# Gated delta net, chunk matrices: the values' factor on ScalarE, the rate's factor of the lower matrix on GpSimd a stage earlier

## The reference, cut to what matters

```python
decay = jnp.exp(jnp.where(incl, gc[..., :, None] - gc[..., None, :], -jnp.inf))
kb = k * beta[..., None]
vb = v * beta[..., None]
L = jnp.where(strict, jnp.einsum('bhncd,bhnsd->bhncs', kb, k) * decay, 0.0)
T = lax.linalg.triangular_solve(eye + L, eye, left_side=True, lower=True, unit_diagonal=True)
u = T @ vb
w = T @ (kb * jnp.exp(gc)[..., None])
a_intra = jnp.where(incl, jnp.einsum('bhncd,bhnsd->bhncs', q, k) * decay, 0.0)
kd = k * jnp.exp(gc[..., -1:] - gc)[..., None]
```

## Time and profile before

| | |
|---|---|
| median of 3 runs | 2669.14 us (2658.22 to 2669.57) |
| profiled execution | 2671.5 us, span 2669.5 us |
| instructions | 44222 |
| TensorE busy | 2329.7 us, 87% of the span |
| VectorE busy | 1002.1 us, 38% |
| ScalarE busy | 448.7 us, 17% |
| GpSimd busy | 243.8 us, 9% |
| mean granted TensorE clock | 0.93 of full speed |

### The profile page before, as it was taken

The page is one execution under the profiler, slowest core; times in us unless marked ns, Lnnn a source line. Parts: engine busy times, 40 slices in busy tenths (PEclk is TensorE's granted clock), DMA queues, the critical chain, the costliest instruction groups (busy, mean ns, idle before and its releaser), DMA issues. The chain is left out here.

```text
span 2669.5 us, 44222 instructions
## 1 busy us (share of the span) xinstructions
PE 2329.7 (87%) x18735; PEld 1249.5 (47%) x18735; DVE 1002.1 (38%) x1791; ACT 448.7 (17%) x841; POOL 243.8 (9%) x180
## 2 busy tenths in 40 slices
PE   7989958969898995896986997879979979999998
PEld 3543417634364441862433442379744444444442
DVE  1166685332116667523224452274331152111112
ACT  1021431010102142101021333212110020000000
POOL 0112210000011221000001560210000000000000
PEclk9989979979899997997987998889989979999999
DMA  4111050020212105002011101100104239999997
GB/s 151 52 63 65 16 209 3 22 80 32 91 52 71 63 9 209 3 22 79 32 63 40 48 17 52 67 3 5 34 33 150 107 151 406 421 421 422 422 422 312
DMA packets 60439, 328.25 MB, mean 123 GB/s; under 512 B 6880, under 2 KB 9440, under 8 KB 31200
## 3 DMA queue, kind: packets, MB, share of 16 engines
q1 hardware_dynamic: 60256, 325.63, 31.4%
HBM read 320.88 MB, written 4.72 MB: 122 GB/s over the span
## 5 line engine op out<-in xcount | busy, mean ns | idle before, releaser
L418 PE MATMUL ps<-store,side_ring 128*128 128x512 f32 x928 | 454.4, 623 | 22.5 <-DMA side_ring<-in_w_rwkv 6.3
L418 PEld LDWEIGHTS ps<-store,side_ring 128*128 128x128 f32 x928 | 166.8, 195 | 205.7 <-issue 179.8
L2192 PE MATMUL ps<-expert_ring,xe 128*64 128x512 f32 x1024 | 223.3, 593 | 2.8 <-DVE back L2301 1.7
L333 PE MATMUL ps<-store,side_ring 128*128 128x512 f32 x384 | 170.9, 608 | 1.9 <-DVE store L299 1.9
L2192 PEld LDWEIGHTS ps<-expert_ring,xe 128*64 128x64 f32 x1024 | 73.0, 137 | 149.6 <-issue 147.5
L333 PEld LDWEIGHTS ps<-store,side_ring 128*128 128x128 f32 x384 | 74.8, 196 | 96.9 <-issue 94.8
L1447 PE MATMUL ps<-store,weight_ring 128*128 128x512 f32 x256 | 112.0, 593 | 1.9 <-DVE store L299 1.9
L2220 PE MATMUL ps<-expert_ring,store 128*64 128x512 f32 x512 | 111.6, 594 | 1.4 <-DVE store L2277 1.4
L1962 PE MATMUL ps<-store,expert_ring 128*128 128x512 f32 x224 | 98.9, 605 | 10.8 <-DMA expert_ring<-in_w_merge 10.8
L546 DVE COPY attn_tok<-ps 128x456 f32<-128x456 f32 (+1 forms) x12 | 6.2, 519 | 237.3 <-PE ps L536 237.3
L418 PE MATMUL ps<-store 128*128 128x512 f32 x160 | 80.1, 656 | 13.7 <-DMA store<-in_w_merge 13.2
(11 more groups left out here) (406 smaller groups left out, 3875.2 us busy)
## 6 DMA issues: line engine op xcount, KB each, us to landing
expert_ring<-in_w_expert SPq DMA_DIRECT2D x192, 1024.0 KB, 16.4
raw<-in_w_ada SPq DMA_DIRECT2D x24, 1024.0 KB, 6.5
side_ring<-in_w_attn SPq DMA_DIRECT2D x34, 512.0 KB, 3.7
side_ring<-in_w_rwkv SPq DMA_DIRECT2D x26, 512.0 KB, 3.6
weight_ring<-in_ple_gate SPq DMA_DIRECT2D x16, 512.0 KB, 3.7
side_ring<-in_w_conv SPq DMA_DIRECT2D x12, 512.0 KB, 3.3
store<-in_w_merge SPq DMA_DIRECT2D x10, 512.0 KB, 3.7
expert_ring<-in_w_merge SPq DMA_DIRECT2D x3, 1536.0 KB, 6.4
```

The source lines that it names most:

```text
L333: last = nc.tensor.matmul(ps[:, u, :], ring[:, u, k, :], src[:, k, :], start=(k == 0), stop=(k == kt - 1))
L418: ins = self.nc.tensor.matmul(self.ps[:, self.banks[j % banks], :], self.ring[:, j % self.slots, k, :], self.src[:, k, :], start=(k == 0), ...
L2192: last = nc.tensor.matmul(ps[w, 2 * ep + half, :], xe[:, ep, k, :], ring[:, unit % SLOTS, k2, S * half:S * half + S], start=(k == 0), stop ...
```

## The change

In the stage of the decays GpSimd waits for its own mask of chunk `n` and then multiplies `low` of that chunk by the rate, broadcast along the columns (semaphore `by_beta`). In the stage of the chunk matrices ScalarE gets a program: per chunk, direction and pair of heads it copies 128x64 of the value bank into `bv` with the rate as its scale, one pair of heads per instruction (semaphore `v_scaled`), and TensorE waits for both `taken` and `v_scaled` of chunk `c - 2`. VectorE keeps three instructions per direction: `low` becomes a scalar_tensor_tensor with the factor -1 in it, `at` and `kd` stay. It waits for its own semaphore once per chunk instead of twice per direction. Each of the two phases has one more semaphore to clear.

```diff
--- before.py
+++ after.py
@@ -1738,7 +1738,7 @@
             block_of = lambda t, n: t[:, n].rearrange("p d j t -> p (d j) t")
             bank8 = lambda i: ps[:, i, :].rearrange("p (b t) -> p b t", b=NB)
             side = beside(5, SPILLED)
-            with phase(nc, rhs_ready=0, spread=0, q_exp=0, capped=0, exp_done=0, masked=0, dve=0,
+            with phase(nc, rhs_ready=0, spread=0, q_exp=0, capped=0, exp_done=0, masked=0, by_beta=0, dve=0,
                        **SpilledProjection.SEMAPHORES) as (block, s):
                 side.attach(s)
 
@@ -1775,7 +1775,10 @@
                         for target, name in ((at, "incl_T"), (low, "strict")):
                             m = M.c(name).rearrange("p (d t) -> p d t", d=2).unsqueeze(2).broadcast_to([P, 2, JP, CH])
                             nc.gpsimd.tensor_tensor(target[:, n], target[:, n], m, ALU.mult).then_inc(s["masked"], 1)
-                    pool.wait_ge(s["masked"], 2 * NCH)
+                        pool.wait_ge(s["masked"], 2 * n + 2)
+                        nc.gpsimd.tensor_tensor(low[:, n], low[:, n], beta[:, n].unsqueeze(3).broadcast_to([P, 2, JP, CH]),
+                                                ALU.mult).then_inc(s["by_beta"], 1)
+                    pool.wait_ge(s["by_beta"], NCH)
 
                 @block.vector
                 def _(dve):
@@ -1792,7 +1795,7 @@
                         nc.vector.tensor_scalar(block_of(low, n), dif[:, n % 2], 0.0, None, ALU.max).then_inc(s["capped"], 1)
 
 
-            with phase(nc, made=0, taken=0, q_scaled=0, dve=0) as (block, s):
+            with phase(nc, made=0, taken=0, v_scaled=0, q_scaled=0, dve=0) as (block, s):
                 bank4 = lambda i: ps[:, i, 0:JP * CH].rearrange("p (j t) -> p j t", j=JP)
 
                 @block.tensor
@@ -1800,6 +1803,7 @@
                     for c in range(NCH):
                         if c >= 2:
                             pe.wait_ge(s["taken"], c - 1)
+                            pe.wait_ge(s["v_scaled"], 2 * JP * (c - 1))
                         here = slice(c * CH, (c + 1) * CH)
                         for j in range(JP):
                             for w in halves:
@@ -1807,6 +1811,15 @@
                                 for i, (lhs, rh) in enumerate(((kc, kc), (kc, qc), (kc, M.c("ident2")[w, :]), (vc, M.c("ident2")[w, :]))):
                                     last = nc.tensor.matmul(bank4(4 * (c % 2) + i)[w, j, :], lhs, rh, start=True, stop=True)
                         last.then_inc(s["made"], 1)
+
+                @block.scalar
+                def _(act):
+                    for c in range(NCH):
+                        act.wait_ge(s["made"], c + 1)
+                        for d, n in ((0, c), (1, NCH - 1 - c)):
+                            for j in range(JP):
+                                nc.scalar.activation(bv[:, n, d, j, :], bank4(4 * (c % 2) + 3)[:, j, :], ACT.Identity,
+                                                     scale=beta[:, n, d, j:j + 1]).then_inc(s["v_scaled"], 1)
 
                 @block.gpsimd
                 def _(pool):
@@ -1823,12 +1836,11 @@
                         b = 4 * (c % 2)
                         for d, n in ((0, c), (1, NCH - 1 - c)):
                             wide = lambda t: t[:, n, d, :].unsqueeze(2).broadcast_to([P, JP, CH])
-                            own.mark(nc.vector.tensor_tensor(low[:, n, d], bank4(b), low[:, n, d], ALU.mult))
+                            own.mark(nc.vector.scalar_tensor_tensor(out=low[:, n, d], in0=bank4(b), scalar=-1.0, in1=low[:, n, d],
+                                                                    op0=ALU.mult, op1=ALU.mult))
                             own.mark(nc.vector.tensor_tensor(at[:, n, d], bank4(b + 1), at[:, n, d], ALU.mult))
                             own.mark(nc.vector.tensor_tensor(kd[:, n, d], bank4(b + 2), wide(decay_out), ALU.mult))
-                            own.step(nc.vector.tensor_tensor(bv[:, n, d], bank4(b + 3), wide(beta), ALU.mult))
-                            own.step(nc.vector.scalar_tensor_tensor(out=low[:, n, d], in0=low[:, n, d], scalar=-1.0, in1=wide(beta),
-                                                            op0=ALU.mult, op1=ALU.mult))
+                        own.settle()
                         dve.sem_inc(s["taken"], 1)
 
         with ExitStack() as stack:
```

## The result

| | before | after |
|---|---|---|
| median, same chip | 2668.9 us (6 runs) | 2651.99 us (2645.47 to 2659.24, 6 runs) |
| ratio, 95% interval | | 0.9945 [0.9929, 0.9961] |
| span of the profiled execution | 2669.5 us | 2652.6 us |

The change makes the kernel 0.55% faster, 14.7 us by the ratio.

The account below looks back on a forecast made before the run. VectorE was taken to bound the chunk-matrix stage, with TensorE next: -13.3 there, +0.15 for GpSimd and +0.14 for semaphores made -13.0 us, from the median 2669.14 to 2656.1. Predicted 2656 us, range 2646 to 2667.

Parts of the forecast that it names:

- VectorE sets the pace before, TensorE after: Chunk matrices: VectorE's 4.07 us a chunk bounds before; afterwards TensorE paces at 4.9 us a pair, 13.3 us less.
- VectorE's price: Chunk matrices: instructions of 0.42 us starting 0.34 us apart, 2.25 us a chunk with waits, bounds 2.1 and 2.9.
- ScalarE's price: Chunk matrices: eight 128x64 copies of 0.33 us, 0.22 to 0.24 apart, 2.0 us a chunk, bounds 1.3 and 2.7.
- TensorE's pairs: Chunk matrices: one chunk of 2.6 us and one of 2.35 make 4.9 us a pair; VectorE ends at 1759.4.
- The clock: Chunk matrices: first chunk at half clock, full clock from 1740 on; one 6.8 us half-clock stretch would give back 3.4 us.
- The possible gain at the head of the inversion: Start of the inversion: first groups sooner by up to 0.7 us if the clock stays up; counted as nothing.
- The decays: End of the decays: GpSimd's last additional product shows by 0.15 us, bounds 0 and 0.95; the other seven cost nothing.
- The sum: Whole kernel: -13.3 for the chunk matrices, +0.15 for GpSimd, +0.14 for two semaphores, giving -13.0 us.
- Rival 4: Chunk matrices: ScalarE becomes a worse bound than VectorE was, from 0.51 us per start; at 0.72, 2683 us; chance 0.05.
- Rival 2: Chunk matrices: ScalarE or VectorE paces at its bound, or a half-clock stretch remains; 2658 to 2660 or 2664 us; chance 0.25.
- rival 3: Clock stays up across the shorter gap and runs fall on their spread's low side; 2645 to 2654 us; chance 0.10.
- case 1: Chunk matrices: TensorE sets the pace, as summed; 2656 us, alone 2654.5 to 2657.5; chance 0.60.

Follow-up runs that it names:

- r3: The change with only the values moved to ScalarE; VectorE keeps the product of `low` with the rate: ratio 0.9971 to the kernel before, stage 32.5 us.
- r4: The changed kernel without ScalarE's program; the values stay with VectorE, only the rate's factor moves to GpSimd: ratio 0.9951 to the kernel before, stage 28.4 us.
- r2: The kernel after, run again without an edit: ratio 0.994 to the kernel before.
- r10: The kernel after, run once more without an edit, on the same chip as the kernel with both stages joined: ratio 0.9958 to the kernel before.
- r7: The changed kernel with one more 128x512 GpSimd product per chunk in the decays: first mask to next stage 48.9 us, one execution without a ratio.
- r1: The kernel before, run again without an edit: ratio 0.9995, span 2668.6 us.
- r6: The changed kernel with each of ScalarE's 128x64 copies cut into four of 128x16: ratio 1.0032 to the kernel before, stage 47.6 us.
- r9: The changed kernel with the decays and chunk matrices in one block, without the barrier between them: ratio 0.9944 to the kernel before, median 2656.96 us.
- r5: The changed kernel with each of ScalarE's 128x64 copies cut into two of 128x32: stage 28.0 us, one execution without a ratio.
- r8: The changed kernel with three needless TensorE products at the end of the decays, shortening its idle time: stage 24.2 us, span 2652.2 us.

## Why the prediction came out as it did

The forecast, 2656 us with 2646 to 2667, holds the measured 2651.99, and the mechanism was the one predicted. Point by point:

- **VectorE sets the pace before, TensorE after.** Shown: VectorE waits in all eight chunks, and r3 and r4, in which VectorE keeps eight instructions, pace at 3.27 and 2.88 us as computed. As in the prediction's steps, each pair of chunks still holds one release by VectorE.
- **VectorE's price.** 0.42 us each and 0.33 to 0.34 apart, as taken; the new form of L1826 costs no more than the old.
- **ScalarE's price.** Predicted 2.0 us a chunk, measured 1.74: starts lie 0.20 us apart instead of 0.24. It has no effect, since it lies under TensorE's 2.45. The Trainium skill ("ScalarE: Activation LUTs", What ACT_TABLE_LOAD costs) has the figures from which, as an estimate, one takes 333 ns and the next starts 93 ns before its end, 240 ns apart. The trace has a median of 0.326 us, which agrees, and starts 0.20 us apart, so the measured overlap is larger, about 0.12 us.
- **TensorE's pairs.** Predicted 4.9 us, measured 4.92. In r2 the eight chunks took 19.12 us from VectorE's first to its last, predicted 19.2; in the first profile 19.84, since the clock rose later.
- **The clock.** As forecast the falls inside the stage are gone, and the first chunk stays at half. Full clock was counted on from the second chunk; in the first profile it came 1.7 us later (0.58 in 1736.20 to 1737.50), which cost nearly all of the 0.8 us between the local times of 30.87 and 30.1. The possible gain at the head of the inversion is small: its first copy to its first `half` took 12.28 us in the first profile after, 12.61 and 12.63 in r2 and r10, against 12.70 and 12.69 before.
- **The decays.** 0.15 us for GpSimd's last product was taken; by r7's comparison it is nothing. The prediction let the stage end when the spill's traffic ended, 1733.5, with 2.2 us for the clears and the barrier; in r7 these take 1.56 us, and counted back from 1735.69 the stage's work in the kernel before ended at about 1734.1, behind the 1733.65 at which GpSimd would have ended. A semaphore more costs 0.08 us (5.50 against 5.41 and 5.42), taken 0.07.
- **The sum.** 13.0 us predicted; the local times give 12.5 to 13.3. The profiles' 16.9 us and the recorded 14.7 are this and the spread outside, which r1 shows without an edit.
- **Rivals.** Rival 4 was built (r6) and is slower than before, as computed. Rival 2 did not occur: neither ScalarE nor VectorE paced at its bound. The recorded median, 2651.99, lies 4 us below the predicted point and in the range of rival 3. It lies outside case 1's own 2654.5 to 2657.5, while the range that the prediction gave holds it. Of rival 3 the clock part is worth 0.4 us in the first profile and 0.1 in the others; the rest is its other part, spread. By the medians the three measurements differ from the kernel before on the same chip by 16.9, 14.6 (r2) and 10.9 us (r10), around the predicted 13.0. So the mechanism and its size were right; where in the range the first median fell is spread, and no merit of the sum.

Which side of 0.5% the change falls on was called open, and still is by its size: 13 us are 0.49%, and the three ratios are 0.9945, 0.994 and 0.9958.

## What to carry to other kernels

Ask for every engine how long it needs for one turn of the loop; the gain of taking work off the slowest ends where the next one begins, so two edits can be worth less together than their sum (5.5 and 9.5 us alone, 12.5 to 13.3 together). In a stage with a barrier on each side, measure the stretch between two fixed instructions in both traces: it repeats to 0.1 us where the clock does (43.39 and 43.40, 30.11 and 30.10 us), while the span moves by 10 us between executions. What remained here after the change lay around the barrier: waiting for a transfer, clearing semaphores, and a first chunk at half clock, together 5.5 us by r9, which doesn't tell them apart.

## What the runs showed of the hardware

- GpSimd beside VectorE changed nothing where VectorE read PSUM (0.69 us in r7, 0.42 in the chunk matrices), and made its tensor_scalar on SBUF up to three times as long (1.31 against 0.42 us, r7): such an instruction ended 0.28 us after the GpSimd product that it met. Products with both operands in SBUF grew as well (L1840 in r3, 0.97 against 0.42 us).
- ScalarE's small instructions hardly get cheaper with their size: starts 0.20, 0.18 and 0.165 us apart for 64, 32 and 16 columns with a pointer scale (the kernel after, r5, r6).
- The granted clock fell while TensorE was working again (r8: full until 1733, half from there, with products since 1731.95), and it stayed full where TensorE had no idle time ahead of the chunks (r9, 1.00 from 1722 to 1756).
